# Output projection of a two-layer decoder trunk: the second 512 features by seven quarter products as well, with the routing behind it in another order

## The reference

```python
h = h + from_heads(o) @ w_out                      # even_mixer / odd_mixer
h = h + hierarchical_moe(rmsnorm(h, ffn_norm[layer]), ...)
...
g_logits = t @ w_group + b_group                   # 4 groups
e_logits = t @ w_router + b_router                 # 32 experts
g_idx = argmax(g_logits); top_v, top_i = top_k(e_logits of that group, 2)
y = sum over chosen experts of gate * (silu(t @ w_gate[e]) * (t @ w_up[e])) @ w_down[e]
```

## Time and profile before

| | |
|---|---|
| median of 3 runs | 1024.78 us (1023.83 to 1028.85) |
| the profiled execution, its own time | 1025.55 us |
| its span, first to last instruction | 1023.7 us |
| mean granted TensorE clock | 0.989 of full speed |
| PE busy (share of the span) | 965.0 us (94%) |
| DVE, ACT, POOL busy | 458.7, 238.7, 184.5 us |
| moved by DMA | 275.73 MB |

### The profile page before, as it was taken

One profiled execution on the slowest core, in us unless ns is written; L12 is line 12 of the kernel. 1 busy time (PEld: TensorE's weight loads), 2 busy tenths in 40 slices (PEclk: granted clock), 3 DMA queues, 4 the chain that ended last, 5 costly groups with the idle time before them and its releaser, 6 DMA issues.

```text
span 1023.7 us, 13907 instructions
## 1 busy us (share of the span) xinstructions
PE 965.0 (94%) x5576; PEld 652.2 (64%) x5576; DVE 458.7 (45%) x1158; ACT 238.7 (23%) x590; POOL 184.5 (18%) x136
## 2 busy tenths in 40 slices
PE   7999999999999899999899999999998999998986
PEld 6888688868556566665444877456755766665542
DVE  5644722386463332222236548677546232222215
ACT  3323700281221000000012226366121100000002
POOL 5540172006001111112103201002401011111100
PEclk9999999999999999999999999999999999999998
DMA  9649502154768999999989220145285999999996
GB/s 334 221 132 206 158 13 105 49 208 170 305 229 312 417 420 418 421 419 420 417 339 277 83 82 2 48 189 209 78 353 206 380 421 418 421 419 420 420 380 258
DMA packets 67026, 275.73 MB, mean 269 GB/s; under 512 B 16067, under 2 KB 20659, under 8 KB 42890
## 3 DMA queue, kind: packets, MB, share of 16 engines
q1 hardware_dynamic: 56960, 257.48, 65.2%
q0 software_dynamic: 10000, 17.34, 4.9%
HBM read 260.64 MB, written 30.44 MB: 284 GB/s over the span
## 4 chain that ended last, share of the span: by engine, by line
PE 72%; DMA 17%; DVE 4%; SPq 3%; issue 2%; POOL 1%; ACT 0%; DVEq 0%; POOLq 0%
PE bank L976 16%; PE bank L1248 12%; DMA K<-rows,small 9%; PE bank L1025 6%; PE bank L1089 6%; PE bank L1262 5%; DMA W<-in_moe_w_up 5%; PE bank L1098 5%; PE bank L1043 3%; PE bank L1059 3%; DMA hnT<-in_moe_w_down 3%; PE bank L1448 3%; SPq L515 2%; PE bank L1270 1%; PE bank L1159 1%
## 5 line engine op out<-in xcount | busy, mean ns | idle before, releaser
L2123 DVE SCALAR_TENSOR_TENSOR PT<-bank,small,PT 128x256 f32<-128x256 f32 x32 | 15.5, 484 | 206.1 <-PE bank L1248 206.1
L1262 PE MATMUL bank<-D,PT 128*64 128x512 f32 x416 | 101.6, 593 | 4.8 <-ACT PT L1696 2.6
L757 POOL DMA_INDIRECT expert_rows<-K,small x30 | 30.3, 1011 | 342.7 <-DVE K L2145 318.0
L1248 PE MATMUL bank<-W,PT 128*64 128x256 f32 x640 | 79.4, 390 | 9.6 <-DMA W<-in_moe_w_up 6.4
L2145 DVE SCALAR_TENSOR_TENSOR K<-K,small,bank 128x512 f32<-128x512 f32 x64 | 47.8, 747 | 86.4 <-PE bank L1262 86.2
L1248 PE MATMUL bank<-W,cst 128*64 128x256 f32 x640 | 78.1, 384 | 0.0
L1696 ACT ACTIVATE PT<-bank 128x256 f32<-128x256 f32 x32 | 12.3, 383 | 263.0 <-PE bank L1254 263.0
L1656 ACT ACTIVATE P<-P,nm 128x128 f32<-128x128 f32 (+5 forms) x128 | 68.3, 536 | 22.1 <-DVE nm L1902 21.6
L1025 PE MATMUL bank<-K,Q 128*128 128x256 f32 (+3 forms) x256 | 70.5, 417 | 1.4 <-DVE nm L1902 1.0
L1248 PEld LDWEIGHTS bank<-W,PT 128*64 128x64 f32 x640 | 50.2, 139 | 33.3 <-issue 10.9
L1262 PEld LDWEIGHTS bank<-D,PT 128*64 128x64 f32 x416 | 36.0, 137 | 48.9 <-issue 43.7
(11 more groups left out here) (314 smaller groups left out, 1804.7 us busy)
## 6 DMA issues: line engine op xcount, KB each, us to landing
D<-in_moe_w_down SPq DMA_DIRECT2D x48, 1024.0 KB, 19.2
W<-in_moe_w_gate SPq DMA_DIRECT2D x40, 1024.0 KB
W<-in_moe_w_up SPq DMA_DIRECT2D x36, 1024.0 KB, 19.4
hnT<-in_moe_w_down SPq DMA_DIRECT2D x12, 1024.0 KB, 17.4
W<-in_e_w_in SPq DMA_DIRECT2D x5, 2048.0 KB
expert_rows<-K SPq DMA_DIRECT2D x2, 4096.0 KB, 35.8
V<-in_moe_w_gate SPq DMA_DIRECT2D x6, 1024.0 KB
Q<-in_moe_w_gate SPq DMA_DIRECT2D x6, 1024.0 KB
```

Of the source, the lines that this page charges most:

```text
L1248: last = nc.tensor.matmul(bank[b][at, 0:256], XT[k // 4][:, k % 4, at], w[:, 256 * k:256 * k + 256], start=(k == 0), stop=(k == KD - 1))
L1262: last = nc.tensor.matmul(bank[5 + half][at, :], hT[:, 128 * c + 64 * a:128 * c + 64 * a + 64], d[:, col:col + 512], start=(c == 0), stop= ...
```

## The change

The second half of the features is computed by seven quarter products too. Its weight sums are taken by POOL in buffer K and in D0 and D1 (`second_weights`, `second_S`), behind those of the first half and ahead of the router loads. Row differences t1 to t4 are used again. Three accumulated parts are copied out of bank 0 by ACT, a fourth is put together from banks 7 and 0 (`second_part`). The products are ordered so that chunks 0 and 1 are complete after five of them; the two products that only chunks 2 and 3 need are cut into a chunk each (`chunk_product`). The router's transposes and products follow in one row, chunk by chunk, in part behind the last product, with `stay_busy` between them. ACT copies both halves of the router's transposes. DVE has the additions, choices and placings in a new order. On SP, the downs of experts 0 to 3 wait for the last product (`s_og` counts 15 a layer now instead of 11), and that of expert 6 follows the up of 5. Ranks move to bank 1, `stay_busy` to bank 7.

```diff
+        second_S = [out_S[0], out_S[1], quarter(D[1][:, 1024:2048])]
+        second_part = [D[1][:, 512:1024], part2, part3, D[1][:, 0:512]]
...
+        def second_weights():
+            w = flatK.rearrange("p (k n) -> p k n", k=KD)
+            return w[:, 0:4, 0:256], w[:, 4:8, 0:256], w[:, 0:4, 256:512], w[:, 4:8, 256:512]
...
         def out_sums_before(lay):
-            return (24, 32)[lay]
+            return (24, 36)[lay]
...
@@ -533,11 +540,8 @@
                 load_cols("K", flatK.rearrange("p (k n) -> p k n", k=KD), w_out, 512, 512)
                 sp.wait_ge(s_pv, 8 * (lay + 1))
                 load_half(lay, 6, 0)
-                sp.wait_ge(s_og, 11 * lay + 7)
+                sp.wait_ge(s_og, 15 * lay + 7)
                 load_gate_up(lay, 4)
-                sp.wait_ge(s_oga, 8 * lay + 4)
-                for e in (0, 1, 2, 6, 3):
-                    load_down(lay, e)
                 rows = h_dram[lay]
                 for c in range(C):
                     sp.wait_ge(s_oga, 8 * lay + 5 + c)
@@ -551,8 +555,11 @@
                         load_half(lay, 7, 0)
                     if c == 1:
                         load_half(lay, 5, 0)
-                sp.wait_ge(s_og, 11 * lay + 11)
+                sp.wait_ge(s_og, 15 * lay + 15)
+                for e in (0, 1, 2, 3):
+                    load_down(lay, e)
                 load_half(lay, 5, 1)
+                load_down(lay, 6)
                 sp.wait_ge(s_hst, 64 * (lay + 1))
                 sp.wait_ge(s_rta, C * (lay + 1))
                 sp.wait_ge(s_rtb, C * (lay + 1))
...
+                pool.wait_ge(*landed("K", ("out", 2 * lay + 1)))
+                a11, a12, a21, a22 = second_weights()
+                s1, s2, s4 = second_S
+                pool.wait_ge(s_og, 15 * lay + 3)
+                nc.gpsimd.tensor_tensor(s1, a21, a22, ALU.add).then_inc(s_wsum, 1)
+                pool.wait_ge(s_og, 15 * lay + 4)
+                pool.wait_ge(s_wsum, before + 5)
+                nc.gpsimd.tensor_tensor(s2, s1, a11, ALU.subtract).then_inc(s_wsum, 1)
+                nc.gpsimd.tensor_tensor(a21, a11, a21, ALU.subtract).then_inc(s_wsum, 1)
+                pool.wait_ge(s_wsum, before + 6)
+                nc.gpsimd.tensor_tensor(s4, a12, s2, ALU.subtract).then_inc(s_wsum, 1)
...
-                w_out = [flatQ.rearrange("p (k n) -> p k n", k=KD), flatK.rearrange("p (k n) -> p k n", k=KD)]
-
-                def product(half, c, k0, k1):
-
-                    g = 8 * lay + 4 * half + c
-                    if k0 == 0:
-                        pe.wait_ge(s_oga, g - 1)
-                    for k in range(k0, k1):
-                        last = nc.tensor.matmul(bank[g % 2][:, :], oT[:, c, k, :],
-                                                w_out[half][:, k, :], start=(k == 0), stop=(k == KD - 1))
-                    if k1 == KD:
-                        last.then_inc(s_og, 1)
+                
+                def chunk_product(b, a, rows, m, starts):
+
+                    for k in range(4):
+                        last = nc.tensor.matmul(b[:, 256 * m:256 * m + 256], rows[:, m, k, :], a[:, k, :],
+                                                start=starts and k == 0, stop=k == 3, skip_group_check=True)
+                    return last
 
                 def quarter_product(b, a, rows, start):
 
-                    for m in range(2):
-                        for k in range(4):
-                            last = nc.tensor.matmul(b[:, 256 * m:256 * m + 256], rows[:, m, k, :], a[:, k, :],
-                                                    start=start and m + k == 0, stop=k == 3, skip_group_check=True)
-                    last.then_inc(s_og, 1)
+                    chunk_product(b, a, rows, 0, start)
+                    chunk_product(b, a, rows, 1, False).then_inc(s_og, 1)
...
@@ -1166,7 +1176,7 @@
                     pe.wait_ge(s_oh, 4 * lay + c + 1)
                     if c:
                         pe.wait_ge(s_facts, 4 * lay + c)
-                    out = bank[7][:, 32 * c:32 * c + 32]
+                    out = bank[1][:, 32 * c:32 * c + 32]
...
                 def stay_busy(times, width):
 
                     for _ in range(times):
-                        nc.tensor.matmul(bank[1][:, 0:width], ident, cst[:, 0:width], start=True, stop=True)
+                        nc.tensor.matmul(bank[7][:, 0:width], ident, cst[:, 0:width], start=True, stop=True)
 
                 first_features()
-                for half, buf in ((1, "K"),):
-                    pe.wait_ge(*landed(buf, ("out", 2 * lay + half)))
-                    for c in range(C):
-                        product(half, c, 0, 1)
-                        if half and c:
-                            first_half(c - 1)
-                            second_half(c - 1)
-                        product(half, c, 1, 3)
-                        if half and c == 3:
-                            slots(0)
-                        if half and c >= 2:
-                            ranks(c - 2)
-                        product(half, c, 3, 4)
-                        if half and c:
-                            logits(c - 1, 0)
-                            logits(c - 1, 1)
-                        if half and c == 3:
-                            first_half(3)
-                        product(half, c, 4, 6)
-                        if half and c == 3:
-                            logits(3, 0)
-                        product(half, c, 6, 8)
+                a11, a12, a21, a22 = second_weights()
+                s1, s2, s4 = second_S
+                t1, t2, t3, t4 = [t.rearrange("p (c k t) -> p c k t", c=2, k=4) for t in o_T]
+                b11, b12, b21, b22 = o_quarters
+                sums, parts = out_sums_before(lay) + 4, 8 * lay + 4
+                pe.wait_ge(*landed("K", ("out", 2 * lay + 1)))
+                quarter_product(bank[0], a11, b11, True)
+                quarter_product(bank[1], a12, b21, True)
+                pe.wait_ge(s_oga, 8 * lay + 4)
+                first_half(0)
+                pe.wait_ge(s_opart, parts + 1)
+                pe.wait_ge(s_wsum, sums + 2)
+                quarter_product(bank[0], s2, t2, False)
+                pe.wait_ge(s_opart, parts)
+                logits(0, 0)
+                quarter_product(bank[2], a22, t4, True)
+                pe.wait_ge(s_opart, parts + 2)
+                pe.wait_ge(s_wsum, sums + 3)
+                quarter_product(bank[0], a21, t3, False)
+                chunk_product(bank[7], s1, t1, 0, True)
+                second_half(0)
+                chunk_product(bank[0], s1, t1, 1, True).then_inc(s_og, 1)
+                logits(0, 1)
+                first_half(1)
+                second_half(1)
+                pe.wait_ge(s_opart, parts + 4)
+                pe.wait_ge(s_wsum, sums + 4)
+                chunk_product(bank[7], s4, b22, 0, False).then_inc(s_og, 1)
+                logits(1, 0)
+                logits(1, 1)
+                first_half(2)
+                chunk_product(bank[0], s4, b22, 1, False).then_inc(s_og, 1)
+                ranks(0)
+                logits(2, 0)
+                second_half(2)
+                stay_busy(1, 512)
+                logits(2, 1)
+                first_half(3)
                 second_half(3)
+                stay_busy(1, 512)
+                logits(3, 0)
+                logits(3, 1)
+                slots(0)
+                ranks(1)
+                stay_busy(3, 512)
                 slots(1)
                 ranks(2)
-                logits(3, 1)
-                stay_busy(2, 512)
+                stay_busy(3, 512)
                 slots(2)
                 ranks(3)
                 stay_busy(1, 256)
...
-                    act.wait_ge(s_og, 11 * lay + at)
+                    act.wait_ge(s_og, 15 * lay + at)
                     nc.scalar.activation(part, b[:, :], ACT.Copy).then_inc(s_opart, 1)
 
+            def second_part_out(lay, n):
+
+                act.wait_ge(s_og, 15 * lay + (8, 10, 12, 13)[n])
+                if n == 3:
+                    nc.scalar.activation(second_part[3][:, 0:256], bank[7][:, 0:256], ACT.Copy)
+                    nc.scalar.activation(second_part[3][:, 256:512], bank[0][:, 256:512], ACT.Copy).then_inc(s_opart, 1)
+                else:
+                    nc.scalar.activation(second_part[n], bank[0][:, :], ACT.Copy).then_inc(s_opart, 1)
+
             def roots_for_router(lay):
 
-                def rows_t_out(c):
-                    act.wait_ge(s_rta, 4 * lay + c + 1)
-                    nc.scalar.activation(rT[0], bank[3][:, :].rearrange("p (k t) -> p k t", k=4), ACT.Copy)\
-                      .then_inc(s_rae, 1)
+                def rows_t_out(c, half):
+                    act.wait_ge((s_rta, s_rtb)[half], 4 * lay + c + 1)
+                    nc.scalar.activation(rT[half], bank[3 + half][:, :].rearrange("p (k t) -> p k t", k=4), ACT.Copy)\
+                      .then_inc((s_rae, s_rbe)[half], 1)
 
```

(91 more changed lines are left out.)

## The result

The changed kernel took 1036.06 us (median of 4 runs, 1035.90 to 1037.01), the one before 1024.86 (4 runs, 1023.83 to 1028.85): ratio 1.0113, interval 1.0095 to 1.0130, some 11.2 us slower. The forecast was 1029.0 with a range up to 1036, on the side of no change; the time lies just outside the range and the side was wrong. The profiled execution took 1037.01 (span 1034.9, mean granted clock 0.984), 11.5 more than that of before.

The account below looks back on a forecast made before the run. DMA bytes were taken to bound the experts' phase: 2.6 us later in layer 0 and 1.3 in layer 1, sum +3.9, plus up to 1 for gathers, gave 1029.0 us, range 1022 to 1036.

Parts of the forecast that it names:

- SP and the DMA stream: Weight loads around the second half: 16.9 us unused against 14.3 and 15.6 before, so layers 2.6 and 1.3 us later.
- 5.3 us after the first gather's landing: Issue of pair 4's first gates: the spacing from before kept, so landing about 314 gives issue at 319.3.
- PE's own path ... adds nothing to the bytes: PE at its first gates: 3.7 us later, but taken up by its existing waits for ups and downs.
- Choices and placings: Routing chain on DVE after logits at 284.2: 19.3 us of work plus gaps, ending 305.8 against 305.7; no gain.
- The sums on POOL and the router weights: Four more POOL sums ahead of the router DMAs: weights land about 265, PE wants the result at 271.6; no cost.
- when that backlog ends: First gather, issued at 306.9 into 5 to 7 us of outstanding prefetch: lands at 314, between 310.3 and 317.5.
- The estimate of 5.9 us: First gather if queues alternate one row per turn: 3.4 + 8 x 0.31 us, landing at 312.8.
- (b): Rival, slower still: first gather takes its loaded 10.6 us, layers +5.8 and +4.5, 1035 us; chance 0.18.
- (c): Rival, no change: DMA stream not binding, PE's 3.8 and 2.6 us waits absorb later first gates, 1025 us; chance 0.20.
- (d): Rival, faster: PE's path alone binds, chain ends earlier by 3.1 us of PE saved a layer, 1018.6 us; chance 0.09.
- (e): Rival: router weights land after 271.6, +1.5 to 4 us a layer on top, 1032 to 1037 us; chance 0.06.
- (a): The forecast itself: bytes decide, +3.9 us and up to 1 for gathers, 1029.0 us, own range 1026 to 1033; chance 0.47.

Follow-up runs that it names:

- PE kept busy: The changed kernel with ten wide matmuls that nobody reads behind the last slots instead of four: 1031.31 us, ratio 1.0050.
- the kernel before with late gates: The kernel before with ten wide matmuls that nobody reads behind the last slots instead of four: 1034.42 us, ratio 1.0099.
- the downs loaded where free: The changed kernel with expert 5's gate and most downs released where their buffers come free, only expert 1's down at the end: 1029.78 us, ratio 1.0044.
- two held: The changed kernel, tiles released where buffers come free, ups of 7 and 5 held behind the first gather, five wide matmuls: 1026.90 us, ratio 1.0019.

## Why the prediction was wrong

**What failed** is the sum in "SP and the DMA stream", +3.9 us for both layers. Its mechanism holds: bytes decide, PE's saving doesn't reach the end. Its size was off by a factor of almost three: the layers took 4.7 and 6.3 us more, not 2.6 and 1.3.

The term that was mis-sized is the empty queue before pair 4's loads, with what sets its end. I let the prefetch run to 319.6 and had pair 4's gates issued at 319.3, "just in time", with nothing unused behind 290 except 0.4. The trace's DMA view from 260.9 to 330 in 40 equal slices (tenths busy, then GB/s; a slice is 1.73 us) shows otherwise:

```profile
DMA  5789910000009991499989999999999891059999
GB/s 60 62 375 339 368 76 0 9 0 0 0 38 405 320 394 57 168 263 394 415 339 398 422 389 446 427 413 436 417 434 387 306 410 71 9 152 455 417 270 417
```

The 34th to 36th slice, 318 to 323, are nearly empty (71, 9, 152 GB/s): the stream had finished 1.6 us sooner than laid out, which costs nothing by itself, and pair 4's gates came 1.5 later, which does. From 315 to 325 the share was 0.60, 4.0 us unused where I had put none. The forecast's 2.6 with these 1.5 would be 4.1 for layer 0, near the 4.7. The first hole was laid out as 14.4 us from 266 on; it was 0.73 x 15 = 11.0, because expert 4's two tiles lasted until about 269.5, in part for the router loads beside them (without those, with only SP's order moved, they were through 6.7 us after their issue, here after some 8.7). It held hardly more bytes for that, the same two tiles.

The 1.5 us come from "5.3 us after the first gather's landing": I moved the whole of before's tail with the gather. Before, four transposes stood on the chain for 0.72 and the gates took 3.67. After, PE had idled 5.47 us for the gather; the granted clock read 0.66 from 310 to 320, a mean of its levels of 1.2 and 2.4 GHz (0.50, the lower one, from 312 to 318), eight transposes took 1.97 and the gates 4.90, 6.9 us in all from landing to the end of the gates. That a later gather lengthens PE's idle time, and so what follows it, was nowhere in my sum. The kernel with PE kept busy shows its worth, 4.75 us of the 11.2. Then "PE's own path ... adds nothing to the bytes" was wrong too: the path sets when the next loads are issued, and in the kernel before with late gates 5.75 and 3.6 us on it cost 9.8 us.

In layer 1 the 1.45 MB that are missing account for 3.5 us of the 6.3. The lower clock at the end of the experts' phase doesn't explain the rest. After PE's last wait for the full stream, sixteen downs took 5.35 instead of 3.65, at a granted clock of 0.68:

```profile
997.00:1002.30 5.30, 5.30 (x17) 1.76 (x17) 0.75 (x1) 0.00 (x0) 0.00 (x0) 0.68 0.98 397
```

But the kernel before loses the same 1.7 there, in both layers; its last wait is for ups, and the 32 gate instructions behind it took 5.36 instead of 3.67. This is its chain in layer 1:

```profile
980.18 5.36 PE bank L1248 x32
```

So 2.8 us of layer 1 stay open, of the same kind as in the other kernels with the new order of PE, DVE and ACT (the table above).

**What held.** The last product at 290.7: exact. Choices and placings: the fourth choice ended at 302.4 (forecast 303.5), the last placing at 304.5 (305.8), the gather issued at 305.49 (306.7). The sums on POOL and the router weights cost nothing: sums to 258.1 (257.6), chunk 0's logits at 271.66 right behind a product, with no wait. Downs released at 292.96 behind chunk 3's store. The gather landed at 313.86 where I had taken 314; in layer 1 it took 7.77. The time was right by luck: the reason, "when that backlog ends", is not borne out. With only SP's order moved, some 11 us of a store and tiles were still outstanding at the gather's issue (an estimate: 7.5 MiB from about 300.2 on), the DMA engines were full until pair 4's loads came, and the gather took 8.11 all the same. The estimate of 5.9 us that I drew from the Trainium skill (DMA: Bandwidth & Descriptors, Queues, rings and completion order) took one row for one turn; the section says that an engine drains a whole packet, typically of some 9 to 17 descriptors, before it switches. The 8.4 and 7.8 contradict my estimate, as the 10.6 of the earlier trace rows had suggested, and say nothing against the rule. The Trainium skill's other rule (SBUF — State Buffer, Who interferes with whom) agrees with the trace: the second and fourth new sums took 2.35; the first, which began while DVE subtracted two SBUF tiles until 248.35, took 3.33, and the third, which began at 253.00 under an add that lasted until 253.60, took 2.81.

**The rivals.** (b) gave 1035 and came nearest in time; its cause, a gather of 10.6, didn't happen, but its consequence did, an empty queue of some 4 us before pair 4's loads, by 8.4 of gather and 1.6 of clock. (c), stream not binding, falls by the table above. My sign for the forecast, more than 3.8 us of waiting for the last ups, was badly chosen as well: PE waited 2.0, for downs, and the layer was late all the same. (d) falls: with early gates and no late bytes the engines' order gained 2.4, not 6.2, since the choices bound the chain as laid out. (e) didn't occur: the router weights had landed by 270.64, before 271.6. Slower got only 0.40 because two thirds of (a) lay below the bound; but gather, clock and empty queue add up, and don't exclude each other as the rivals did.

## What to carry to other kernels

Where both PE and the DMA engines are full in the long phase, cost a change in the short phase before it by the megabytes moved until the stream is full, and ask first what releases the next loads: here a kernel that was changed in nothing but its first gates, 5.75 and 3.6 us later in the two layers, lost 9.8. Loads that must wait for a buffer should not all be queued ahead of a small transfer that the next work waits for; send each when its own buffer is free (6.3 us here). When a wait grows, the work behind it is priced anew at the clock that the engine will have after idling, and cover for it should be as long as the wait and no longer (five matmuls against ten: 6.0 us).

## What the runs showed of the hardware that was unexpected

- A gather of 128 rows of 4 KiB landed 3.6 us after its issue with the queue nearly empty, 5.6 with part of the prefetch outstanding, 8.4 and 7.8 with an estimated 6 to 7 us of it, and 8.1 with some 11. It did not wait for the backlog's end.
- In these places the granted clock fell after PE had idled for 2.0 to 5.5 us. What followed the longest: 32 instructions in 4.90 us for 3.67, eight transposes in 1.97. After shorter waits for weights near the end of an experts' phase: sixteen downs in 5.35 for 3.65, and in the kernel before 32 gates in 5.36 for 3.67. Not after every such wait: in layer 1 of "two held" PE waited 2.79 us for downs, and the sixteen behind it took 3.65. With the downs loaded where free, four transposes after a wait of 2.71 still took 0.72 and the gates behind them 5.29: the clock fell only after PE had begun again.
- Six small loads of router weights were issued together with 2 MiB of weights. The DMA engines moved 60 GB/s in the first 1.7 us, as without them (77 in the kernel before), but also in the next 1.8 (there 357), though seven tenths busy. The two tiles were through some 2 us later than in a kernel without the small loads beside them.
